# Layer norms from moments gathered during the projection, partition sums in quarters, and two weight chunks multiplied together behind a norm

## The reference

```
def layer_norm(x, g, b):
    mu = mean(x, -1);  var = mean(square(x - mu), -1)
    return (x - mu) * rsqrt(var + 1e-5) * g + b
def rmsnorm(x, g):
    return x * rsqrt(mean(x * x, -1) + EPS) * g
# block 1, layer i: mixer -> layer_norm -> conv_ffn -> layer_norm
g = h @ w_gate; g = conv3(g); out = (silu(g) * (h @ w_up)) @ w_down
# block 2: rmsnorm -> @ w_in -> SSD and short convolution -> @ w_out
#          -> rmsnorm -> 16 experts, top 2 -> final rmsnorm
```

## Time and profile before

| | us |
|---|---|
| median of 3 runs | 1902.23 (1898.44 to 1902.69) |
| the profiled execution | 1903.71 |
| its span in the trace | 1901.7 |
| TensorE matmuls busy | 1759.4 (93%) |
| VectorE busy | 1074.3 (56%) |
| ScalarE busy | 822.1 (43%) |
| mean granted clock of TensorE | 0.959 of full speed |

### The profile page before, as it was taken

The page is one execution under the profiler, slowest core; times in us unless marked ns, Lnnn a source line. Parts: engine busy times, 40 slices in busy tenths (PEclk is TensorE's granted clock), DMA queues, the critical chain, the costliest instruction groups (busy, mean ns, idle before and its releaser), DMA issues.

```text
span 1901.7 us, 23130 instructions
## 1 busy us (share of the span) xinstructions
PE 1759.4 (93%) x9368; PEld 1371.0 (72%) x9368; DVE 1074.3 (56%) x1587; ACT 822.1 (43%) x1162; POOL 0.9 (0%) x5
## 2 busy tenths in 40 slices
PE   4988999899999989899888999889999989999996
PEld 1744446577787767589558999779877857877775
DVE  2255663544433432542876756546766645888886
ACT  2334442443212321533445545445444424767664
POOL 0000000000000000000000000000000000000000
PEclk7999999999999989999989999989999977999999
DMA  9211333044334442132103454424321306989993
GB/s 373 87 44 45 111 111 133 22 177 177 140 115 174 162 173 101 47 131 82 52 3 129 163 206 160 162 94 150 134 89 67 134 22 238 366 324 354 339 332 126
DMA packets 42239, 287.64 MB, mean 151 GB/s; under 512 B 4736, under 2 KB 5888, under 8 KB 10640
## 3 DMA queue, kind: packets, MB, share of 16 engines
q1 hardware_dynamic: 41952, 285.97, 41.4%
q10 hardware_dynamic: 144, 0.06, 0.0%
q0 software_dynamic: 32, 0.07, 0.0%
HBM read 285.03 MB, written 1.05 MB: 150 GB/s over the span
## 4 chain that ended last, share of the span: by engine, by line
PE 82%; DVE 9%; ACT 5%; issue 2%; DMA 2%; DVEq 0%; ACTq 0%
PE ps L475 16%; PE ps L477 16%; PE ps L476 16%; PE ps L2352 5%; PE ps L2322 2%; PE ps L1285 2%; PE ps L2326 2%; PE ps L2323 2%; PE ps L501 2%; DVE WL L465 2%; DMA ring<-wts 2%; PE ps L2258 2%; PE ps L1254 1%; PE ps L1186 1%; PE ps L576 1%
## 5 line engine op out<-in xcount | busy, mean ns | idle before, releaser
L475 PE MATMUL ps<-HH,WH 128*128 128x512 f32 (+2 forms) x1552 | 524.1, 338 | 36.7 <-DVE HL L650 19.6
L477 PE MATMUL ps<-HH,WL 128*128 128x512 f32 (+2 forms) x1552 | 509.0, 328 | 0.0
L476 PE MATMUL ps<-HL,WH 128*128 128x512 f32 (+2 forms) x1552 | 508.4, 328 | 0.0
L465 DVE TENSOR_TENSOR WL<-ring,WH 128x2048 fp32r<-128x2048 f32 (+2 forms) x191 | 413.4, 2171 | 165.6 <-ACT WH L455 165.3
L455 ACT ACTIVATE WH<-ring 128x2048 fp32r<-128x2048 f32 (+2 forms) x191 | 347.4, 1819 | 324.2 <-PE ps L477 178.8
L475 PEld LDWEIGHTS ps<-HH,WH 128*128 128x128 f32 x1552 | 299.5, 193 | 91.8 <-issue 53.0
L476 PEld LDWEIGHTS ps<-HL,WH 128*128 128x128 f32 x1552 | 299.7, 193 | 24.1 <-issue 1.9
L477 PEld LDWEIGHTS ps<-HH,WL 128*128 128x128 f32 x1552 | 299.0, 193 | 23.6
L693 DVE SCALAR_TENSOR_TENSOR X<-ps,modv,X 128x256 f32<-128x256 f32 x72 | 32.6, 481 | 162.7 <-PE ps L477 162.5
L475 PE MATMUL ps<-parts,WH 128*128 128x512 f32 (+1 forms) x352 | 123.1, 350 | 0.0
L476 PE MATMUL ps<-parts,WH 128*128 128x512 f32 (+1 forms) x352 | 119.1, 338 | 0.0
(11 more groups left out here) (324 smaller groups left out, 2186.6 us busy)
## 6 DMA issues: line engine op xcount, KB each, us to landing
ring<-wts SPq DMA_DIRECT2D x206, 1024.0 KB, 5.0
arena<-wts SPq DMA_DIRECT2D x38, 1024.0 KB, 6.6
ring<-wts SPq DMA_DIRECT2D x32, 704.0 KB, 4.1
X<-xin SPq DMA_DIRECT2D x1, 2048.0 KB, 12.8
cst<-csts SPq DMA_DIRECT2D x1, 1373.0 KB, 17.0
ring<-wts SPq DMA_DIRECT2D x3, 384.0 KB, 3.1
out<-arena SPq DMA_DIRECT2D x2, 512.0 KB, 2.9
ring<-wts SPq DMA_DIRECT2D x1, 640.0 KB, 3.5
```

Of the source, the lines that this page charges most:

```text
L465: e.tensor_tensor(lo, raw(i), hi.bitcast(F32), ALU.subtract).then_inc(*up("low", i))
L475: e.matmul(o, w[0][:, cols], x[0], start=k == 0, stop=False)
L476: e.matmul(o, w[0][:, cols], x[1], start=False, stop=False)
L477: return e.matmul(o, w[1][:, cols], x[0], start=False, stop=k == nk - 1)
```

## The change

1. **Moments during the projection.** After tile 0 of an output projection, its mean over 128 features of block 0 is taken as a shift; DVE subtracts it from all 8 blocks of X (`dve_shift`, between tiles 2 and 3). While the later tiles run, ACT squares each finished block and TensorE adds both first and second moment. Behind the last tile the variance is second moment minus squared mean; the mean itself is subtracted in the loop that scales. The table load of the root is taken ahead of the last squares.
2. **Quarters.** Each sum over partitions is four matmuls with 32 columns of weights, one per quarter of the tokens, to four groups of 32 PSUM partitions (`pe_sums`); root and reciprocal then work on a quarter of the columns, and four matmuls with 128 columns bring a row back to all partitions (`pe_spread`). The three rms norms take the same path.
3. **Two chunks together.** Behind n00, n01, n10 and mix, `four_tiles` takes the four tiles of the first two chunks block by block.
4. In n00 and n01, ACT applies scale and shift to both halves. In mix, DVE squares each block as soon as it is final.

```diff
+        def four_tiles(e, cs, o, x, names, arrive):
+            ws = [weights(e, c) for c in cs]
+            for k in range(8):
+                e.wait_ge(*at(*arrive, k))
+                for c, w, oc, name in zip(cs, ws, o, names):
+                    for m in range(2):
+                        t = mm3(e, oc[m], w, ..., at_k(x, k), k, 8)
...
+        def pe_sums(e, b, ones, x, q, start, stop):
+            for g in range(4):
+                t = e.matmul(ps[32 * g:32 * g + 32, b, 0:q], C(ones, 32), x[:, q * g:q * g + q], start=start, stop=stop)
+        def pe_spread(e, b, x, q):
+            for g in range(4):
+                t = e.matmul(ps[:, b, q * g:q * g + q], ident[:, 32 * g:32 * g + 1].to_broadcast([128, 128]), x,
...
+        def pe_moments(e, N, j):
+            e.wait_ge(*(at("center", tag, j) if j < 3 else at("y", tag, j)))
+            pe_sums(e, b[0], "o1024", X[:, j, 0:N.n], N.q, ...)
+            e.wait_ge(*at("square", tag, j))
+            pe_sums(e, b[1], "o1024", N.SQ[:, j % 3, :], N.q, ...)
...
+        def pe_out_sums(e, N, j):
+            if j == 1:
+                pe_shift_sums(e, N)
+            elif j == 2:
+                pe_shift(e, N)
+            elif j == 3:
+                pe_moments(e, N, 0)
+                pe_moments(e, N, 1)
+            elif j == 4:
+                pe_moments(e, N, 2)
+                pe_moments(e, N, 3)
+            elif j > 4:
+                pe_moments(e, N, j - 1)
...
         def dve_norm(e, N, y, full=True):
+            e.tensor_copy(N.MU, B("moment", tag, 0)[:, 0:q])
+            e.tensor_tensor(N.RS, N.MU, B("moment", tag, 0)[:, 0:q], ALU.mult)
+            e.tensor_tensor(N.VR, B("moment", tag, 1)[:, 0:q], N.RS, ALU.subtract)
+            e.reciprocal(N.RS, N.VR)
...
+            center(0)
+            center(1)
+            unit = B("unit_dev", tag)[:, 0:n]
             for j in range(9):
                 if j < 8:
-                    e.tensor_tensor(N.T8[:, j, :], y[:, j, :], N.RS, ALU.mult)
+                    e.tensor_tensor(N.T8[:, j, :], y[:, j, :], unit, ALU.mult)
+                    center(j + 2)
...
         def pe_ffn(e, F_):
+                if half == 0:
+                    four_tiles(e, [index["gu", l, f] for f in range(2)], ..., ("norm_low", F_.arrive))
...
         def pe_diff_inputs(e):
+            four_tiles(e, [index["din", 4 + i] for i in range(2)], ..., ("norm_low", "n01"))
...
         def pe_win(e):
+            four_tiles(e, [index["win", i] for i in range(2)], ..., ("u_low",))
```

More of the change, by code:

```diff
@@ L569, in __init__ @@
             def __init__(self, tag, n):
[L570 to L576, removed]
+                self.tag, self.n, self.q = tag, n, n // 4
+                self.HB, self.T8 = area(3, n), area(8, n)
@@ new lines, in pe_shift_sums, with pe_shift @@
+        def pe_shift_sums(e, N):
+            b = bank(e, "shift_sums", N.tag)
+            e.wait_ge(*at("y", N.tag, 0))
+            pe_sums(e, b, "o128", X[:, 0, 0:N.n], N.q, True, True).then_inc(*up("moments.shift_sums", N.tag))
+            banks.give(b, "shift_row", N.tag)
+        def pe_shift(e, N):
+            b = bank(e, "shift", N.tag)
+            e.wait_ge(*at("shift_row", N.tag))
+            pe_spread(e, b, N.SH, N.q).then_inc(*up("moments.shift", N.tag))
+            banks.give(b, "center", N.tag, 7)
+            for i in range(2):
+                bank(e, "moment", N.tag, i)
@@ L579, in pe_mean @@
-                banks.give(banks.of["mean", tag], "center", tag, 7)
+                banks.give(b[0], "variance.square", tag)
+                banks.give(b[1], "variance", tag)
         def pe_norm(e, N):
[L582 to L587, removed]
+            b = bank(e, "mean", N.tag)
@@ new lines, in pe_norm, with act_shift @@
+            e.wait_ge(*at("variance.mean", N.tag))
+            pe_spread(e, b, N.MU, N.q).then_inc(*up("mean", N.tag))
+            banks.give(b, "scaled.centered", N.tag, 7)
+            b = bank(e, "unit_dev", N.tag)
+            e.wait_ge(*at("variance.inverse", N.tag))
+            pe_spread(e, b, N.RS, N.q).then_inc(*up("mean.unit_dev", N.tag))
+            banks.give(b, "scaled", N.tag, 7)
+        def act_shift(e, N):
+            e.wait_ge(*at("moments.shift_sums", N.tag))
+            e.activation(N.SH, B("shift_sums", N.tag)[:, 0:N.q], ACT.Copy).then_inc(*up("shift_row", N.tag))
@@ L589, in act_norm, with act_squares @@
+        def act_squares(e, N, j):
+            tag = N.tag
+            e.wait_ge(*(at("center", tag, j) if j < 3 else at("y", tag, j)))
+            if j >= 3:
+                e.wait_ge(*at("moments", tag, j - 3))
+            e.activation(N.SQ[:, j % 3, :], X[:, j, 0:N.n], ACT.Square).then_inc(*up("square", tag, j))
         def act_norm(e, N, y, full=True):
             tag, n = N.tag, N.n
[L591 to L595, removed]
@@ L596, in act_norm @@
-            e.wait_ge(*at("var", tag, 7))
-            e.activation(N.SD, B("var", tag)[:, 0:n], ACT.Sqrt, bias=EPS5, scale=1.0).then_inc(*up("root.dev", tag))
+            e.wait_ge(*at("variance", tag))
+            e.activation(N.VR, N.VR, ACT.Sqrt, bias=EPS5, scale=1.0).then_inc(*up("root.dev", tag))
             if not full:
@@ L619, in act_residual, with dve_shift @@
                          bias=lnc[:, 1, j:j + 1]).then_inc(*up("residual", N.tag, j))
-        def dve_norm(e, N, y, full=True):
-            tag, n = N.tag, N.n
-            e.wait_ge(*at("mean", tag))
[L624 to L629, removed]
+        def dve_shift(e, N, before):
+            e.wait_ge(*at("moments.shift", N.tag))
+            for j in range(8):
+                e.wait_ge(*(at(*before, j) if j > 2 else at("y", N.tag, j)))
+                e.tensor_tensor(X[:, j, 0:N.n], X[:, j, 0:N.n], B("shift", N.tag)[:, 0:N.n],
+                                ALU.subtract).then_inc(*up("center", N.tag, j))
@@ L647, in dve_norm @@
+                    e.tensor_tensor(N.T8[:, j, :], y[:, j, :], unit, ALU.mult).then_inc(*up("scaled", tag, j))
+                    center(j + 2)
                 if j:
@@ L691, in dve_out @@
                         e.wait_ge(*at(*nxt, j))
+                    if j > 2 and tag in NORMS:
+                        e.wait_ge(*at("center", tag, j))
                     for s, a, z in halves(n):
@@ L760, in act_ffn @@
                     act_mod(e, 1, 23)
-                act_out(e, ("down", l, half), 1)
+                act_out(e, ("down", l, half), 1, F_.tag if half else None)
         def dve_ffn(e, F_, gt_from, fold_next=None):
@@ L2164, in over @@
             return a.unsqueeze(2).to_broadcast([128, 3, n])
+        STAT_ROWS = {"mix": sc_root[:, 0:NT // 4], "ffn": RSTD[:, 0:NT // 4], "fin": RSTF[:, 0:NT // 4]}
         def dve_first_max(e, src, m, h, name):
@@ L2623, in scalar_program @@
             act_heads(e)
-            act_out(e, ("about",), 2)
+            act_out(e, ("about",), 2, "n00")
             act_norm(e, N00, X)
```

198 lines of the change are left out of this document (125 added, 73 removed).

## The result

| | before | after |
|---|---|---|
| median of 4 runs, us | 1900.34 (1898.2 to 1902.69) | 1937.38 (1935.35 to 1938.87) |
| span of the profiled execution, us | 1901.7 | 1937.1 |
| mean granted clock of TensorE | 0.959 | 0.943 |

The ratio is 1.0187, 95% interval 1.0168 to 1.0206: 37 us slower where 34 were forecast, and 1937.4 where 1936 was.

A forecast was written before the change was run, and what follows sets the result against it. TensorE is full between norms, so time can be won only at the norms, where it stands. 4.4 + 16.7 + 4.7 + 11.5 - 1.5 - 1.8 = +34 us, giving 1936 us, range 1918 to 1952.

The forecast's parts named there:

- Two chunks together: Behind four norms: TensorE waits for the second chunk's low part, behind the last `norm_low`; n00 +16.7, n01 +4.7, n10 +11.5.
- n00: Norm with 512 tokens: late start and an 8.5 us stall before the third chunk, +16.7 us (14.8 wait, 1.9 clock).
- n01: Norm ahead of the `din` chunks: start 22.2 us behind the last y, no second stall, +4.7 us.
- n10: Norm with 256 tokens: later third chunk (+9.6) plus 1.9 for the clock behind a 5 us stall, +11.5 us.
- mix: Norms n11 and mix: shorter norms, but TensorE waits for the last block and a split of `win` 1; -1.5 us.
- sums in the stream: In the projections: quarter sums replace whole means, +0.2 us each with 512 tokens, +2.0 with 256; +4.4 in all.
- ffn, fin and all else behind mix's first matmul: Last norms: ffn -0.5 us from sums in its stream, fin -1.3 from sums, root and reciprocal less spread; together -1.8.
- low bound: Quarter sums in the projections: a group costs its columns alone, 0.1 to 0.2 us, taking 8 us off the forecast.
- dear sums: Rival, quarter sums: loads and issues, not columns, set a group's cost of 1.07 us; +37, 1973 us; 10%.
- second chunk in time: Rival, at the norms: the second chunk's low part is done before the norm's first block; 1890 us; 4%.
- no second stall: Rival, n00 and n10: the third chunk comes in time, so 10.4 and 6.8 us fall away; 1919 us; 8%.

The follow-up runs named there:

- e2_two: The changed kernel with part 3 undone at all four places, one chunk by blocks as before; 1880.9 us, ratio to before 0.9900.
- e3_four_only: The kernel before with part 3 alone (`four_tiles` at its four places and the matching order of steps on the keys); 1962.71 us, ratio 1.0323.
- e7_warm: The changed kernel with unused float32 products filling TensorE's waits at n00, n01 and n10; 1933.46 us, ratio to before 1.0155.
- e1_early: The changed kernel with the second chunk's split moved ahead of the norm; 1896.76 us, ratio to before 0.9973.
- e4_mod_first: The changed kernel with layer 0's first `mod` chunk ahead of the four tiles instead of behind them; one run, 1935.28 us.
- e6_din_win: The changed kernel with two chunks together only at n01 and mix, their split ahead, feed-forwards one chunk by blocks; 1880.31 us, ratio to before 0.9881.
- e8_whole: e2_two with whole sums and full-width rows in the four layer norms, rms norms still on quarters; 1906.22 us, ratio to before 1.0018.

## Why the prediction was right

The mechanism is as forecast, step by step. Times behind T:

| | forecast | measured |
|---|---|---|
| n00: first, last `norm_low` done | 8, 19.8 | 7.5, 19.5 |
| n00: start, end of two chunks, third chunk | 23.4, 47.5, 58.2 | 23.1, 47.3, 57.6 |
| n01: start, end of two chunks | 22.2, 46.3 | 21.9, 46.7 |
| n10: start, end, third chunk | 14.7, 29, 33.9 | 14.8, 28.1, 33.0 |
| mix: start | 24.1 | 23.9 |

And by the terms of its sum, in us of the two traces, rounded (the sums in the stream from the first y to T, at n10 from the projection's first matmul):

| term | forecast | measured |
|---|---|---|
| sums in the stream, n00, n01, n10, n11 | 0.2, 0.2, 2.0, 2.0 | 0.3, 0.3, 1.3, 1.4 |
| n00, n01, n10 | 16.7, 4.7, 11.5 | 16.2, 5.2, 11.1 |
| mix | -1.5 | -1.7 |
| ffn, fin and all else behind mix's first matmul | -1.8 | -0.1 |
| stretches that the forecast left out | 0 | 1.3 |
| in all | 34 | 35.4 |

Each term is within 1.7, but part of the closeness of the total is luck: misses of both signs cancel.

- **Two chunks together** was the deciding step, and the one that e2_two and e3_four_only isolate. That the low part of the second chunk would be the releaser came from the order of the queues, its time from the earlier trace rows, and the third chunk's from the earlier trace rows. The terms: n00 +16.7 forecast, +16.2 to the `mod` behind the third chunk; n01 +4.7 against +5.2 (22.5 - 17.3); n10 +11.5 against +11.1 by the last y of the first half of that feed-forward (1126.80 before, 1162.55 after), 8.6 of it (33.3 - 24.7) at the third chunk's start, where 9.6 was forecast, and the rest with the slow clock behind that.
- n10's end was put 0.9 late: I took 2.85 us for the clock from the longer of the earlier trace rows, and 1.9 would have been right. Two chunks took 13.3 with 11.4 of work. At n01 it was the other way: 1.9 were taken for the clock, the two chunks took 24.7 us where 22.2 + 1.9 were forecast, and 21.9 in e7_warm at full clock.
- **Sums in the stream** came to 3.4 us where 4.4 were forecast, by two misses that partly cancel. Two groups with 128 columns lengthen a tile by 0.82 us (6.28 from one pair to the next, less 24 matmuls by 0.2275), as with 0.4 each, but the second pair in a tile adds only 0.39. With 64 columns a pair costs 0.54, and a second pair 0.23. So a group that is not the first in its tile was priced about twice too high. The other misreading goes the other way: seven whole means were taken out ahead of T, but the seventh runs beside the last y (the row at 349.25 in the earlier trace rows is two of them), and only six lay ahead. What went out of a projection is 5.2 us with 512 tokens and 2.5 with 256 (forecast 6.2 and 3.1), what came in is 5.5 and 3.9 (forecast 6.4 and 5.1). The prediction's price for its low bound is off as well: at 0.2 and 0.1 a group, 52 groups give -10 and not -8.
- The rival of **dear sums** is refuted for these shapes: a group costs 0.4 us or less, where it had 1.07. The Trainium skill (TensorE: Matmul & The Clock Gate, The mechanism) says that a weight load overlaps running matmuls only when its row group differs. This trace does not agree: the four matmuls of a group share all 128 rows, and the eight loads of the second group run from 330.63 to 330.87, while matmuls of the same rows run before and beside them (330.50 and 330.74). Rows of PE in after, four groups in a row and then two, with those loads (PEld) in second place:

```profile
330.50 0.42 PE L591 MATMUL ps<-X,cst 128*32 128x128 f32 x8
330.63 0.24 PEld L591 LDWEIGHTS ps<-arena,cst 128*32 128x32 f32 x8
330.74 0.40 PE L591 MATMUL ps<-arena,cst 128*32 128x128 f32 x8
330.96 0.40 PE L591 MATMUL ps<-X,cst 128*32 128x128 f32 x8
331.17 0.40 PE L591 MATMUL ps<-arena,cst 128*32 128x128 f32 x8
...
343.45 0.43 PE L591 MATMUL ps<-X,cst 128*32 128x128 f32 x8
...
349.73 0.43 PE L591 MATMUL ps<-X,cst 128*32 128x128 f32 x8
```

- The rival with the **second chunk in time** (1890 us) had its point of decision right: e1_early moves exactly that, and gives 1896.8. Its price was 7 too good: it put the early split at nothing, and in e1_early the starts at n01, n10 and mix come 2.6, 1.7 and 3.2 us later than the rival had them.
- The rival with **no second stall** did not occur; e4_mod_first shows that an earlier transfer alone would not have brought it about.
- **Behind mix** the forecast had -1.8. The last norm, fin, gives its part (16.9 us from the product before it to the end, where before has 18.1), but from mix's first matmul to that product after takes 634.8 us and before 633.7. The 0.5 of ffn does not show, and the cause of the 1.1 stays open.
- **What the prediction did not say**: how good parts 1 and 2 are alone. It gave the norm as "8 to 9 us faster", and e2_two shows 8.3 of that at n00's third chunk (T + 35.1 against T + 43.4). Part 4 was not tried by itself.

## What to carry to other kernels

When a consumer is made to wait for two things at once, look in the queues for what the second one stands behind: here the work was ready earlier and the wait longer, because the second chunk's split sat behind the whole norm. A slow first step that hides later preparation is worth its time, and batching it can pay only if that preparation is moved as well; even then it gained nothing where it was tried (n01 and mix in e6_din_win), and the moved preparation was not free. Of a change in parts, try each part alone: e2_two, the change without its third part, is 1% faster than before, while the whole is 1.9% slower.

## What the runs showed of the hardware

- Four matmuls to four groups of 32 PSUM partitions go side by side: as a second pair in a tile, a quarter group costs 0.20 us with 128 columns and 0.12 with 64, where one whole sum of 512 takes 0.85 (e8_whole, 352.65 to 353.50).
- DVE's reciprocal goes by columns: 3.35 us for 512, 0.95 for 128, 0.55 for 64 in e2_two at n11. Of the 4.8 us by which e2_two starts earlier behind T of n00 than e8_whole, 2.4 are this.
- Keeping TensorE busy in a wait held its clock at 1.00 there, but not always afterwards. With 2.2 us idle between the fill and the work (n01) it stayed at 1.00; with 2.6 and 2.7 us (n00 and n10) it fell to 0.50 for some 3 us, about 1 us after work had begun. These are three cases, and no run shows where the limit lies. Behind the unfilled wait of 18.9 us at n00 in after it was 0.50 from the first matmul on for 4.5 us, and behind 17.7 us at n01 for 6.1.
